# Two transformer blocks on one core: half 0's turns before half 1's norm, the state output normalised by halves, the last stage read from PSUM

## The reference, cut to what matters

```python
h = rmsnorm_2(x, pre_norm_w)
...
o_a = moba_attention(partial_rope(heads(q_a), pos), partial_rope(heads(k_a), pos), heads(v_a))
y_a = jnp.einsum('bse,ed->bsd', o_a * jax.nn.silu(z_a), w_branch_a)
...
o_b = rmsnorm_2(o_b, gdn_norm_w).reshape(bsz, s, GDN_VWIDTH).astype(x.dtype)
y_b = jnp.einsum('bse,ed->bsd', o_b * jax.nn.silu(z_b), w_branch_b)

merged = jax.nn.sigmoid(gate_a) * y_a + jax.nn.sigmoid(gate_b) * y_b
out = jnp.einsum('bsd,de->bse', merged, w_out)
return x + rmsnorm_2(out, post_norm_w)
```

## Time and profile before

| | us |
|---|---|
| median of three runs | 1508.53 |
| the runs | 1506.31 to 1513.41 |
| the profiled execution's own time | 1503.67 |
| its span, first to last instruction | 1501.9 |
| mean granted TensorE clock, as a share of 2.4 GHz | 0.923 |

### The profile page before, as it was taken

How to read it: one execution, slowest core, us unless ns; L and a number is a source line. 1 busy time by engine, 2 the same in 40 slices (tenths; PEclk the granted TensorE clock), 3 DMA queues, 4 the chain that set the end, 5 groups by cost and what they waited for, 6 DMA issues and landing times.

```text
span 1501.9 us, 13765 instructions
## 1 busy us (share of the span) xinstructions
PE 1175.3 (78%) x5016; PEld 688.0 (46%) x5016; DVE 759.3 (51%) x1743; ACT 483.6 (32%) x1254; POOL 362.5 (24%) x285
## 2 busy tenths in 40 slices
PE   5898876866867776666577767599897789999896
PEld 1687644422412221111122211156775579999782
DVE  2312457968479954465444454511667764431212
ACT  1022122644333433344332333312885441111101
POOL 0688101223434434334333344100000000000000
PEclk9898788988999998999989998999999999999998
DMA  9764404779999999999999999645321130204130
GB/s 337 287 257 169 162 22 160 272 281 394 413 415 420 412 398 413 422 422 421 422 396 399 400 401 422 271 141 196 113 100 68 57 112 1 91 29 162 56 112 28
DMA packets 91870, 377.49 MB, mean 251 GB/s; under 512 B 6323, under 2 KB 9564, under 8 KB 58972
## 3 DMA queue, kind: packets, MB, share of 16 engines
q0 software_dynamic: 36864, 268.45, 43.9%
q1 hardware_dynamic: 53152, 103.98, 19.1%
q10 hardware_dynamic: 1788, 4.19, 0.9%
HBM read 375.54 MB, written 1.06 MB: 251 GB/s over the span
## 4 chain that ended last, share of the span: by engine, by line
PE 43%; DVE 23%; DMA 22%; ACT 8%; issue 2%; POOL 1%; SPq 0%; DVEq 0%; POOLq 0%; ACTq 0%
PE ps L87 43%; DMA AR<-in_puv,idx 20%; DVE AR L87 11%; DVE RT L87 3%; ACT L87 3%; DVE acc L87 3%; DMA W<-in_w_mod 2%; DVE rowb L87 2%; ACT av L87 1%; ACT acc L87 1%; ACT AR L87 1%; DVE hT L87 1%; ACT rowb L87 1%; DVE tok L87 1%; POOL AR L87 1%
## 5 line engine op out<-in xcount | busy, mean ns | idle before, releaser
L87 PE MATMUL ps<-AR,acc 128*64 128x512 f32 x952 | 366.1, 689 | 196.6 <-ACT acc L87 195.5
L87 POOL DMA_INDIRECT AR<-in_puv,idx x256 | 270.3, 1056 | 528.5 <-PE ps L87 405.7
L87 PE MATMUL ps<-hT,W 128*128 128x256 f32 (+2 forms) x1504 | 319.8, 370 | 3.7 <-ACT acc L87 1.9
L87 PEld LDWEIGHTS ps<-AR,acc 128*64 128x64 f32 x952 | 88.7, 148 | 452.6 <-ACT acc L87 371.7
L87 PEld LDWEIGHTS ps<-hT,W 128*128 128x128 f32 (+1 forms) x1504 | 267.9, 194 | 54.5 <-issue 13.6
L87 DVE CUSTOM_DVE_ANT_0 AR<-AR,mixT 128x1024 f32<-128x1024 f32 x128 | 156.7, 1226 | 155.6 <-DMA AR<-in_puv,idx 155.3
L87 DVE CUSTOM_DVE_ANT_0 AR<-AR,tok 128x1024 f32<-128x1024 f32 x128 | 153.3, 1221 | 64.2 <-DMA AR<-in_puv,idx 64.2
L87 ACT ACTIVATE av<-av 128x1 f32<-128x1 f32 x256 | 51.3, 200 | 321.2 <-DVE av L87 321.1
L87 ACT ACT_TABLE_LOAD x103 | 132.1, 1283 | 16.9 <-issue 15.1
L87 PE MATMUL ps<-W,hT 128*128 128x512 f32 (+3 forms) x288 | 95.5, 488 | 0.0
L87 ACT ACTIVATE acc<-fold,av 128x64 f32<-128x64 f32 x238 | 82.8, 348 | 7.8
(11 more groups left out here) (223 smaller groups left out, 1143.4 us busy)
## 6 DMA issues: line engine op xcount, KB each, us to landing
W<-in_w_in SPq DMA_DIRECT2D x25, 2048.0 KB, 7.8
W<-in_w_mod SPq DMA_DIRECT2D x12, 2048.0 KB, 16.7
W<-in_w_out SPq DMA_DIRECT2D x2, 2048.0 KB, 10.2
W<-in_wq SPq DMA_DIRECT2D x2, 2048.0 KB, 10.2
AR<-in_puv,idx POOLq DMA_INDIRECT x256, 11.3
W<-in_wba SPq DMA_DIRECT2D x2, 2048.0 KB, 7.7
W<-in_wbb SPq DMA_DIRECT2D x2, 2048.0 KB, 7.6
W<-in_wo SPq DMA_DIRECT2D x2, 2048.0 KB, 7.7
```

Of the source, the lines that this page charges most:

```text
L87: ins = f(*args, **kw)
```

## The change

Three edits. The block that finishes half 1 of the first block, with its norm, is moved behind the two turns of half 0. In the state output, `finish_o` for a half's second group now also takes that half's root, reciprocal and product over its eight heads, and `zb_step(2)` is moved from in front of half 1's new values to behind half 1's output, next to `zb_step(3)`. In the last stage ScalarE no longer copies the products: it takes Square of each bank with the row's sum (its elementwise output in `ow` is written over later); VectorE adds the two sums, ScalarE takes the root, VectorE the reciprocal, and then for each 512 columns VectorE multiplies the bank's content by it and the norm's weight, adds x, and SP stores 256 KB.

```diff
--- before.py
+++ after.py
@@ -1247,12 +1247,6 @@
         t_pelast = e
 
 
-        for _ in x2_steps(1, t_pelast, t_rot["k", 0]):
-            pass
-        t_xb = t_xb2[1]
-        t_, t_tp = norm_T((1,), tok_at, [t_xb], PV[:, V_PRE:V_PRE + 8], None, [])
-        t_hb.append(t_)
-        t_hball = t_hb[0] + t_hb[1]
         at[0] = 0
         gfree = t_gfree
         vA = ar(2 * D).rearrange("p (a d) -> p a d", a=2)
@@ -1283,6 +1277,12 @@
 
         rope_turn("q", 0)
         rope_turn("k", 0)
+        for _ in x2_steps(1, t_pelast, t_rot["k", 0]):
+            pass
+        t_xb = t_xb2[1]
+        t_, t_tp = norm_T((1,), tok_at, [t_xb], PV[:, V_PRE:V_PRE + 8], None, [])
+        t_hb.append(t_)
+        t_hball = t_hb[0] + t_hb[1]
         for n in range(2):
             qk_project("q", 1, n, [t_tp])
         for n in range(2):
@@ -1708,6 +1708,7 @@
             return e
 
         sqfree = []
+        t_on = []
         osq = sb("osq", [P, 16])
 
         def finish_o(b, t, a, g4):
@@ -1719,6 +1720,12 @@
                       accum_out=osq[:, 4 * n + hh:4 * n + hh + 1], after=[e2] + sqfree[hh:hh + 1])
                 sqfree[hh:hh + 1] = [e]
             t_ob[n] = [e, t]
+            if g4 == 1:
+                q = osq[:, 8 * a:8 * a + 8]
+                e = A(act, q, q, ACT.Sqrt, scale=1.0 / 128, bias=eps, after=[e])
+                e = V(rec, q, q, after=[e])
+                o = ob[:, 8 * a:8 * a + 8, :]
+                t_on.append(V(tt_, o, o, q.unsqueeze(2).to_broadcast([P, 8, P]), MUL, after=[e]))
 
         t_vn, t_s1 = {}, {}
         for g4 in range(2):
@@ -1750,7 +1757,6 @@
             e = V(tt_, r, r, b.t[:, :].rearrange("p (h e) -> p h e", h=4), SUB, after=[t, t_M[2 + g4, "v"]])
             b.free = [e]
             t_vn[1, g4] = [r, e]
-        zb_step(2)
         for g4 in range(2):
             t_vn[1, g4] = new_values(1, g4, t_vn[1, g4][0], [t_vn[1, g4][1]])
         for g4 in range(2):
@@ -1762,17 +1768,15 @@
                 t = PE(mm, b.t[:, hh * 128:hh * 128 + 128], QTv[1][:, h, :], vn[:, 2 + g4, hh, :], start=False, stop=True,
                        after=[t_vn[1, g4], t_Q[2 + g4]])
             finish_o(b, t, 1, g4)
+        zb_step(2)
         zb_step(3)
-        t = A(act, osq[:, :], osq[:, :], ACT.Sqrt, scale=1.0 / 128, bias=eps, after=[t_ob[3][0]])
-        t = V(rec, osq[:, :], osq[:, :], after=[t])
-        t_on = V(tt_, ob[:, :, :], ob[:, :, :], osq[:, :].unsqueeze(2).to_broadcast([P, 16, P]), MUL, after=[t])
         t_obT = []
         obT = zbT
         for h2 in range(4):
             b = ps.take()
             for q in range(4):
                 h, a = 2 * h2 + q // 2, q % 2
-                t = PE(tr, b.t[:, q * 128:q * 128 + 128], ob[:, 8 * a + h, :], ident, after=b.old + [t_on])
+                t = PE(tr, b.t[:, q * 128:q * 128 + 128], ob[:, 8 * a + h, :], ident, after=b.old + t_on)
             o = obT[:, 2 * h2:2 * h2 + 2, :].rearrange("p h t -> p (h t)")
             e = V(stt, o, b.t[:, :], PV[:, V_GN:V_GN + 1], o, MUL, MUL,
                   after=[t] + t_zb)
@@ -1783,24 +1787,30 @@
 
 
         ow = tok2
-        t_o = [[], []]
         wo = [next_w(), next_w()]
+        s_out = dsem("s_out")
+        ends = []
         for a in range(2):
+            bs, sq = [], []
             for n in range(2):
                 i, w, t_w_ = wo[n]
                 b = ps.take()
                 t = token(w, 0, 512, mT, a, t_w_, [t_mg[h] for h in (0, 2, 4, 6)], b, 0)
-                e = A(act, ow[:, a, n * 512:n * 512 + 512], b.t[:, :], ACT.Copy, after=[t, t_on])
-                b.free = [e]
-                t_o[a].append(e)
-        s_out = dsem("s_out")
-        ends = []
-        for a in range(2):
-            t = rms(ow[:, a, :], D, st[:, 18 + a:19 + a], t_o[a])
-            t = V(stt, ow[:, a, :], ow[:, a, :], st[:, 18 + a:19 + a], R_POST, MUL, MUL, after=[t, t_rows[1]])
-            t = V(tt_, ow[:, a, :], ow[:, a, :], X[:, a, :], ADD, after=[t])
-            ends.append(SP.dma(nc.sync.dma_start, s_out, out[a * P:a * P + P, :], ow[:, a, :], after=[t]))
-        SP.wait(*ends)
+                v = st[:, 22 + 2 * a + n:23 + 2 * a + n]
+                sq.append(A(act, ow[:, a, n * 512:n * 512 + 512], b.t[:, :], ACT.Square, accum_out=v, after=[t] + t_on))
+                bs.append(b)
+            r = st[:, 18 + a:19 + a]
+            e = V(tt_, r, st[:, 22 + 2 * a:23 + 2 * a], st[:, 23 + 2 * a:24 + 2 * a], ADD, after=sq)
+            e = A(act, r, r, ACT.Sqrt, scale=1.0 / D, bias=eps, after=[e])
+            e = V(rec, r, r, after=[e])
+            for n in range(2):
+                c = slice(n * 512, n * 512 + 512)
+                o = ow[:, a, c]
+                t = V(stt, o, bs[n].t[:, :], r, R_POST[:, c], MUL, MUL, after=[e, t_rows[1]])
+                bs[n].free = [t]
+                t = V(tt_, o, o, X[:, a, c], ADD, after=[t])
+                ends.append(SP.dma(nc.sync.dma_start, s_out, out[a * P:a * P + P, c], o, after=[t]))
+        SP.wait(ends[-1])
 
         queues = (PE, V, A, G, SP)
         for q in queues:
```

## The result

| | before | after |
|---|---|---|
| median of five runs each, us | 1512.33 | 1499.57 |
| the runs | 1506.31 to 1513.41 | 1494.27 to 1500.9 |
| the profiled execution's own time | 1503.67 | 1500.9 |
| its span | 1501.9 | 1499.1 |

The ratio after to before is 0.9925 (95%: 0.9902 to 0.9948), while the two medians alone give 0.9916; the forecast, 1497.0 over 1508.53, was 0.9924. The change is faster by 0.75%, and the time lies in the range.

What follows compares the result with a forecast made beforehand. TensorE's matmuls were taken to bound the kernel, with 43% of the span. Gains of 0, 6.3 and 5.2 sum to 11.5 us (ends 7.5 and 13.4), taking 1508.53 to 1497.0; range 1492 to 1503.5.

Steps and rivals of the forecast that it cites:

- Part 2: State output by halves: TensorE's stop of 4.92 us goes and transposes run faster; 6.3 us gained, ends 4.7 and 6.6.
- The clock's share: State output's 16 transposes: without a stop the clock stays high, 1.8 us in place of 3.44, 1.65 gained.
- The bared evacuations: State output: moving zb_step(2) uncovers VectorE's subtractions; cost 0.2 us for both steps, ends 0 and 1.8.
- cover: State output: half 1's product ready by 1388, TensorE at the transposes at 1396.5, so 8 us to spare.
- Part 3: Last stage: 4.65 us from the shorter chain behind the last matmul, 0.6 from the smaller store; 5.2 gained in all.
- Part 1: Half 0's turns ahead of half 1's norm: 0 us gained, ends +1.3 and -0.6.
- 1.7 to 2.3 are lost: Projections behind half 1's norm: us lost to the low clock, against 2.15 gained by starting earlier.
- as long as at the two restarts shown: Projections behind the norm: the clock was assumed to return 3.4 to 4.6 us after they begin.
- part one is wrong: Sign at the projections: they start at 979.8 with the clock high, or it stays low for over 5 us.
- the turns pay in full: Rival at half 1's norm: clock returns early or hole is smaller; 2.1 us more gained, 1494.9; chance 0.15.
- The covered gain: Rival: bared evacuations cost 1.8, Square needs a reload, last store no sooner; 7.5 us gained, 1501.0; chance 0.15.
- The clock never stayed low: Rival: new 0.95 us hole behind the norm keeps projections at 1.2 GHz, up to +60 us, 1557; chance 0.02.

Runs made afterwards that it cites:

- e7: Kernel before plus five unread products in the stop ahead of the state output's transposes; transposes 1.80 us instead of 3.44, state output 84.87 instead of 86.50; one run.
- e1: Kernel before with only half 0's turns moved ahead of half 1's norm; ratio to before 0.9994 (0.9980 to 1.0009).
- e4: Kernel before with only the new last stage; ratio to before 0.9967 (0.9952 to 0.9982).
- e3: Kernel before with only the state output by halves and zb_step(2) moved; ratio to before 0.9950 (0.9933 to 0.9967).
- e8: Changed kernel with one 512 KB store per half in place of two of 256 KB; tail 35.17 us against 34.53; one run.
- e10: The changed kernel measured once more, unaltered; ratio to before 0.9903 (0.9881 to 0.9925).
- e2: Changed kernel with half 1's norm put back in front of half 0's turns; ratio to before 0.9902 (0.9885 to 0.9919).
- e5: Changed kernel plus six unread products between half 0's turns and half 1's norm; ratio to before 0.9902 (0.9883 to 0.9921).
- e11: Changed kernel with eight unread products behind the queries' turn and the keys' turn moved behind the norm; ratio to before 0.9905 (0.9881 to 0.9929).

## Why the prediction was right

**Part 2, 6.3 predicted, 6.62 in the profiled pair.** The stop of 4.92 went whole. The clock's share was 1.69 (3.44 less 1.75), for 1.65; e7 has 1.63. The bared evacuations cost little, as taken: the steps from 1384.69 to 1386.53 and on to 1388.41 are 1.84 and 1.88, 0.15 together above the 1.78 and 1.79 of before, for 0.2; the end of 1.8 can be struck. Half 1's product is over at 1397.29 (the row below), which is the predicted 1388 plus the 9.21 us by which this stretch lies later in this execution (1384.69 against 1375.48), and TensorE comes to the transposes at 1405.80: 8.5 us of cover, for 8. Two of the untouched state outputs, in e1 and e4, took 87.15 and 87.19, because there the low clock reached into the gate's first 32 matmuls (7.69 in e1, for 7.07); so the part is worth up to 0.7 us more than the profiled pair shows. Part 2 is shown for the edit as a whole; whether it needed the halves stays open, as said at e3. VectorE's product of half 1 in after:

```profile
1396.07 1.22 DVE L87 TENSOR_TENSOR mixT<-mixT,osq 128x1024 f32<-128x1024 f32 x1
```

**Part 3, 5.2 predicted, 5.39 measured.** VectorE ends 4.37 us behind the last Square's start (1492.31 to 1496.68), for 4.4: 4.67 less than before. The span ends 2.42 later, where it was 3.14: 0.72 for the store, for 0.6. Square needs no table load beside the root. The table loads show no drain: at 1479.29 a load of 1.28 is followed by the root 0.01 behind it. By the Trainium skill (ScalarE: Activation LUTs, section "What ACT_TABLE_LOAD costs") a switch costs some 1.38 more, a drain; the trace does not agree, as it did not before.

**Part 1, 0 predicted, -0.74 in the profiled pair, no difference in e1's timed runs.** The mechanism was right: the hole in front of the projections got 2.07 us shorter, for 2.15, and the clock took it back. The size of the term "1.7 to 2.3 are lost" was too small at its upper end: the 96 matmuls lost 2.81 in the profiled execution, 2.36 in e1, 1.71 in e8 and 1.64 in e10 against 41.20. The step that failed is "as long as at the two restarts shown", 3.4 and 4.6 us: in the changed kernel the clock came back 5.5 us behind the projections' start, and 3.2 in e10 (low for 10.2 us both times, but from a later moment in the changed kernel), so the same instructions give different delays, and the prediction's own sign for "part one is wrong", over 5 us, was met there. What held the 0 is that the loss lies around the gain, not that it equals it. The Trainium skill (TensorE: Matmul & The Clock Gate, section "What's actually happening") has activity as what releases the throttled state, and the traces agree: at this place the clock rose only behind unbroken work on TensorE (5.5 us of it in the changed kernel, 3.2 in e10, 4.6 before).

Smaller steps: the four copies took 2.07 together, where four times 0.60 was taken, since they overlap; so the root was not even 0.1 late (E to root 4.21 in both).

**The rivals.** That the turns pay in full fell with the profiles: the block is 54.64 on average with both turns in front and 54.87 in the old order, 0.2 of the 2.1. The timed runs can't exclude it: 2.1 us would be 0.9986, inside e1's 0.9980 to 1.0009, and e2 is not told from the changed kernel. The covered gain (7.5) fell with each of its three costs: evacuations 0.15, no reload, a store 0.64 sooner. The clock never stayed low for more than 5.5 us of projections. That the edit doesn't do what it says fell with the rows: the turns stand right behind E.

**The size of the whole.** The forecast was within 0.01% of the measured ratio, and 0.08% from that of the medians. That is luck: the sum's three terms were 0.74 too high, 0.3 and 0.2 too low, and the changed kernel measured again gave 0.9903 for 0.9925.

## What to carry to other kernels

Moving work from behind a stall into it shortens the stall, but if that work was also what ran while the clock came back, what stands behind it now pays the same time; look at the granted clock behind the hole before counting the gain. What waits in an engine's queue behind another part's work is the cheapest thing to find and to mend: a root behind the next half's copies was worth 4 us, and the state output's root, behind a SiLU that waited for TensorE, stood in a stop of 5 (there the order was changed together with the split by halves, so their shares are open). And where a long stretch ahead varies from run to run, read a change from landmarks near it, not from the spans.

## What had not been expected

In e5 the clock fell to 1.2 GHz for 3.4 us behind two stops as short as 1.42 and 0.88 us, with TensorE working between them, while with one of 0.58, behind unread products of 512 columns in the hole (8 in the program, 7.03 us), it held at 2.4 GHz (e11). These are one profile each. In the last expert steps, where stops of 1.4 and 0.55 us alternate, it fell at 973.5 in after and held at 2.4 GHz from 941 to E in before; so such stops can stand before a fall and need not, and what decides was not found.

The stretch up to E, whose instructions are the same in all kernels, ended between 968.57 and 977.26 us. That is more than any part of the change, and more than the half width of the intervals, some 0.2% or 3 us. In after the clock was low there, too: the last six expert matmuls took 3.55, where before they took 1.93. What makes it vary was not tried.
